# A hybrid decoder trunk on one core: a 25th place for expert weights, a reordered tail, and the third branch's value products a quarter earlier

## The reference

```python
def mixer_block(...):
    xn = rms_norm(x, norm_g)
    proj = xn @ w_in                       # 1024 x (5120 + 8 + 3072)
    y_sb = ...                             # stick-breaking attention, 8 heads x 64
    y_mb = ...                             # block-sparse attention, 8 heads x 64
    y_ml = mlstm_chunkwise(...) * sigmoid(ml_o)   # matrix memory, 4 heads x 128
    y = jnp.einsum("nbsw,nwd->nbsd", branches, w_branch)      # 3 x (512 x 1024)
    merged = jnp.einsum("bsnd,nbsd->bsd", gates, y)
    return x + merged @ w_out

def hier_moe_block(...):
    xn = rms_norm(x, norm_g)
    # softmax over 4 groups takes one; softmax over its 8 experts takes two
    hid = silu(einsum("nd,edf->nef", xn, w1)) * einsum("nd,edf->nef", xn, w3)
    hid = hid * combine                    # 32 experts, inner width 256
    return x + einsum("nef,efd->nd", hid, w2)
```

## Time and profile before

| | us |
|---|---|
| median of 3 executions | 991.89 |
| lowest and highest | 991.26, 992.02 |
| the profiled execution, whole | 992.2 |
| its span in the profile | 990.1 |
| PE busy in the span | 946.0 (96%) |
| PE weight loads | 758.8 (77%) |
| DVE busy | 483.8 (49%) |
| ACT busy | 419.2 (42%) |
| POOL busy | 27.1 (3%) |
| moved by DMA | 293.36 MB |

### The profile page before, as it was taken

One profiled execution on the slowest core, in us unless ns is written; L12 is line 12 of the kernel. 1 busy time (PEld: TensorE's weight loads), 2 busy tenths in 40 slices (PEclk: granted clock), 3 DMA queues, 4 the chain that ended last, 5 costly groups with the idle time before them and its releaser, 6 DMA issues.

```text
span 990.1 us, 19050 instructions
## 1 busy us (share of the span) xinstructions
PE 946.0 (96%) x8004; PEld 758.8 (77%) x8004; DVE 483.8 (49%) x894; ACT 419.2 (42%) x645; POOL 27.1 (3%) x43
## 2 busy tenths in 40 slices
PE   8999999999999999977999999999999999998886
PEld 8898899999876566544698988999998756564544
DVE  7466875477833222222273669655687422232111
ACT  7465654656542221111275565564754421211111
POOL 1011000000000000000100110000000000000000
PEclk9999999999999999989999999999999999999989
DMA  8734545557799999999975264536769999999995
GB/s 288 272 126 170 177 171 170 192 193 298 290 391 402 422 421 420 419 420 421 382 242 198 87 218 157 185 128 213 274 237 365 381 389 421 420 420 420 420 421 212
DMA packets 86310, 293.36 MB, mean 296 GB/s; under 512 B 17040, under 2 KB 17104, under 8 KB 61904
## 3 DMA queue, kind: packets, MB, share of 16 engines
q1 hardware_dynamic: 86224, 292.12, 76.8%
HBM read 291.05 MB, written 1.05 MB: 295 GB/s over the span
## 4 chain that ended last, share of the span: by engine, by line
PE 75%; DMA 14%; DVE 4%; ACT 3%; SPq 1%; issue 1%; ACTq 0%; DVEq 0%
PE ps_a L854 10%; PE ps_a L856 10%; PE ps_a L855 10%; PE ps_b L1186 9%; DMA units_over_xnT<-in_w_dram 6%; PE ps_a L838 5%; PE ps_a L840 5%; PE ps_a L839 5%; PE ps_b L1207 4%; PE ps_b L1134 3%; DMA unit_from_layer_begin<-in_w_dram 3%; DMA weight_ring<-in_w_dram 3%; DMA units_over_splits<-in_w_dram 3%; PE ps_b L1299 2%; PE ps_a L1258 2%; SPq L605 1%
## 5 line engine op out<-in xcount | busy, mean ns | idle before, releaser
L1614 DVE TENSOR_TENSOR w_low<-weight_ring,w_high 128x1024 fp32r<-128x1024 f32 x167 | 201.3, 1230 | 91.9 <-ACT w_high L1330 91.4
L1330 ACT ACTIVATE w_high<-weight_ring 128x1024 fp32r<-128x1024 f32 x166 | 173.6, 1057 | 156.4 <-PE ps_a L856 107.2
L854 PE MATMUL ps_a<-xnT_high,w_high 128*128 128x256 f32 x704 | 200.8, 285 | 0.1
L856 PE MATMUL ps_a<-xnT_high,w_low 128*128 128x256 f32 x704 | 199.0, 283 | 0.0
L855 PE MATMUL ps_a<-xnT_low,w_high 128*128 128x256 f32 x704 | 198.1, 281 | 0.0
L854 PEld LDWEIGHTS ps_a<-xnT_high,w_high 128*128 128x128 f32 x704 | 132.8, 189 | 2.4 <-issue 2.4
L855 PEld LDWEIGHTS ps_a<-xnT_low,w_high 128*128 128x128 f32 x704 | 133.1, 189 | 0.5 <-issue 0.5
L856 PEld LDWEIGHTS ps_a<-xnT_high,w_low 128*128 128x128 f32 x704 | 131.9, 187 | 0.0
L1540 ACT ACTIVATE h<-ps_b 128x256 f32<-128x256 f32 x64 | 24.5, 383 | 142.9 <-PE ps_b L1186 142.9
L1993 DVE TENSOR_TENSOR y_lo<-ps_b,y_hi 128x512 fp32r<-128x512 f32 x30 | 20.8, 692 | 105.8 <-ACT y_hi L1571 105.8
L1299 PEld LDWEIGHTS ps_b<-fold_two_matrices,h 128*128 128x128 f32 x256 | 35.0, 196 | 40.3 <-issue 36.1
(11 more groups left out here) (372 smaller groups left out, 1758.7 us busy)
## 6 DMA issues: line engine op xcount, KB each, us to landing
weight_ring<-in_w_in_dram SPq DMA_DIRECT2D x62, 1024.0 KB, 5.2
units_over_splits<-in_w_dram SPq DMA_DIRECT2D x48, 1024.0 KB, 23.1
units_over_attention<-in_w_dram SPq DMA_DIRECT2D x40, 1024.0 KB, 21.9
weight_ring<-in_w_dram SPq DMA_DIRECT2D x24, 1024.0 KB, 20.8
units_over_xnT<-in_w_dram SPq DMA_DIRECT2D x20, 1024.0 KB, 22.4
units_over_merged<-in_w_dram SPq DMA_DIRECT2D x16, 1024.0 KB, 24.3
weight_ring<-in_w_branch_dram SPq DMA_DIRECT2D x12, 1024.0 KB, 5.4
unit_from_layer_begin<-in_w_dram SPq DMA_DIRECT2D x10, 1024.0 KB, 18.4
```

The costliest lines, as they stand in the source:

```text
L854: mm(dst, wh, xh, start=row == 0 and s % 2 == 0, stop=False, skip_group_check=True)
L856: last = mm(dst, wl, xh, start=False, stop=row == rows - 1, skip_group_check=True)
L1330: A(mix_buf(whi, i), mix_raw(i), ACT.Copy).then_inc(hi_ready, 1)
L1614: v.tensor_tensor(mix_buf(wlo, i), mix_raw(i), mix_buf(whi, i).bitcast(F32), ALU.subtract).then_inc(lo_ready, 1)
```

## The change

The change has six parts.

1. **A 25th place.** `ONCE_UNITS` becomes `(4, 5, 23, 24)`. The new place `unit_over_choice` lies over tiles of the router and over four constants (`tri`, `neg_mask`, `trineg_r`, `negones_r`) and `w_router`, which are moved next to each other for it. It takes the unit with order number 24, a w2 matrix. SP loads it after `unit_over_x`, waiting for the first of the weighted selections (`selw_ready`, DVE line 1919), and before it reads the number of rounds. The loop then has 71 loads.
2. **Constants again.** Since the place overwrites the four constants, POOL builds them again in layer 1 (`constants_again`, eight instructions on tiles of 128x128), and PE and DVE wait for them (`begun` at 11) before they use them.
3. **Moved tiles.** `selectT0` now lies in the place of unit 5 too, so ACT copies it only in the pair p = 1 (`first_selT_out`, waiting until unit 5 is used), and in that pair `outputs(0)` stands before the gathers. The tiles `hid`, `h`, `silu_h1` and `h3_weighted` move elsewhere.
4. **Tail.** `last_y` of the first half comes before the last scatter, and the `idle_work(3)` before that scatter and the `idle_work(2)` before `last_y` are gone (five matmul groups in all).
5. **`ml_out`** moves a quarter earlier, to stand after quarter 1 of branch 1.
6. **Layer 1's first part.** POOL makes `w_low` of the first part in two instructions of half the size, the second of them only after all of the new x is scaled (`xs_ready`), and DVE's wait for it moves one step later.

```diff
-ONCE_UNITS = (4, 5, 23)
+ONCE_UNITS = (4, 5, 23, 24)
+CONSTANTS_AGAIN = 11
...
+    once_choice = Region(nc, one_b.at, whole.at).sb("unit_over_choice", [P, UNIT])
...
-            steps.append(("first_selT", 0))
             selecting.extend((1, piece, 0) for piece in range(3))
+        elif p == 1:
+            steps.append(("first_selT_out", 0))
+            outputs(p - 1)
+            gather()
...
         hidden_T(2 * p + 1)
         if last:
+            steps.append(("last_y", (len(order), 0)))
             steps.append(("scatter", p - 1))
         select_next()
-    steps.extend(("last_y", (len(order), half)) for half in range(2))
+    steps.append(("last_y", (len(order), 1)))
...
                 load_unit(sp, ONCE_UNITS[2])
+                sp.wait_ge(selw_ready, 1)
+                load_unit(sp, ONCE_UNITS[3])
...
+    def constants_again(pool):
+        def below(buf, row, fill):
+            nc.gpsimd.affine_select(out=buf[:, :], in_=buf[:, :], compare_op=ALU.is_ge, fill=fill, base=0,
+                                    pattern=[[row, P]], channel_multiplier=-row).then_inc(begun, 1)
...
-            nc.gpsimd.tensor_tensor(mix_buf(wlo, 0), mix_raw(0), mix_buf(whi, 0).bitcast(F32),
-                                    ALU.subtract).then_inc(lo_ready, 1)
-
-            pool.wait_ge(xs_ready, NT)
+            for k in range(2):
+                if k:
+                    pool.wait_ge(xs_ready, 2 * NT)
+                low = nc.gpsimd.tensor_tensor(mix_buf(wlo, 0)[:, k, :], mix_raw(0)[:, k, :],
+                                              mix_buf(whi, 0)[:, k, :].bitcast(F32), ALU.subtract)
+            low.then_inc(lo_ready, 1)
...
+        if l:
+            pool.wait_ge(lo_ready, 10)
+            constants_again(pool)
...
-        branch(1, [1, 2]); ml_out(); branch(1, [3]); branch(2)
+        branch(1, [1]); ml_out(); branch(1, [2, 3]); branch(2)
...
-                pe.wait_ge(first_taken, 2)
+                pe.wait_ge(first_taken, 1)
...
-                    if p == PAIRS - 2:
-                        idle_work(3, ps_h)
...
                     if half == 0:
-                        idle_work(2, ps_h)
...
-                elif what == "first_selT":
+                elif what == "first_selT_out":
                     act.wait_ge(first_given, 2)
+                    act.wait_ge(unit_used, used[ONCE_UNITS[1]])
...
-        if l:
-            dve.wait_ge(lo_ready, 1)
         for b in range(4):
+            if l and b == 1:
+                dve.wait_ge(lo_ready, 1)
...
+            if l:
+                dve.wait_ge(begun, CONSTANTS_AGAIN)
```

45 lines of the change are left out of this document (30 added, 15 removed).

## The result

The changed kernel took 982.71 us (median of 4 executions, 982.44 to 984.56) beside 991.58 us for the kernel before (4 executions, 989.42 to 992.02): a ratio of 0.9902 with a 95% interval of 0.9882 to 0.9923.

The account below looks back on a forecast made before the run. DMA streams were taken to bound the expert stretches, chained waits between engines the mixers. Gains of 1.6 (ml_out), 2.45 (place), 0.2 (tail) and 0.1 (layer 1's start) sum to 4.35 us: 987.5 us from 991.89, range 985.0 to 990.4.

Parts of the forecast that it names:

- ml_out: Mixer of each layer: moving it a quarter earlier removes PE's wait before branch 2, 0.79 us a layer, 1.6 in all.
- The place: Expert streams: the 25th place fills dips where loads wait on `unit_used`, 2.45 us in all, bounds 0 and 5.0.
- The tail: End of each layer: reordered last steps without idle matmuls gain 0.2 us, all in layer 1, bounds 0 and 0.4.
- Layer 1's start: Start of layer 1: halving POOL's 2.38 us instruction frees DVE's first sum of squares sooner, 0.1 us gained.
- The constants: Layer 1: POOL's eight rebuilding instructions lie beside other work and cost 0, at most 1.5 us.
- the upper bound of that step: Constants in layer 1: one DVE split held up by the whole length of its POOL neighbour, 1.5 us.
- The place gives nothing: Rival, expert streams: dips come from slow transfers, not a missing place, so 990.0 us; chance 0.15.
- The change does not do what it says: Rival, expert loads: the place's wait comes too late and holds back the reloads; result between the first two rivals; no separate chance.
- A whole unit: Rival, expert streams: each stream starts one unit ahead, 5.0 us in place of 2.45, so 985.0 us; chance 0.13.
- The clock: Rival, both tails: PE idling drops the clock, matmuls take twice as long, 10.4 us more, so 997.9 us; chance 0.06.
- whether a stream makes up a dip by itself: Expert streams: a 435 GB/s ceiling could let a 1 us dip vanish, but the windows stayed at 414 to 418.

Follow-up runs that it names:

- One number: Kernel before with region `one` 36992 bytes long instead of 36960, so the two regions behind it start at multiples of 64: 989.02 us, ratio 0.9965.
- the fourth group: Runs on addresses at multiples of 256: changed kernel with old tail 978.65 us, also without the 25th place 980.40, old kernel 985.02; and gather first in changed kernel 982.77.
- The rest alone: Changed kernel with the ml_out move, the 25th place and the new tail all taken back: 981.91 us, ratio 0.9898.

## Why the prediction was wrong

**`ml_out`: right, a little small.** The step said 0.79 us a layer and that a wait of PE's goes. It is 0.93 to 1.08 in the traces of both pairs of kernels that differ in it alone. The step bounded the gain by the wait that the profile names, and two things in PE's row were not as it took them. In the unchanged kernel the last matmul before branch 2 and its first are 1.07 us apart in their starts, in the kernel that moves `ml_out` alone they are 0.44 us apart. A short wait stays (0.2 us; 0.3 in the changed kernel), and 0.63 us go. And there was a second, smaller pause before quarter 2 of branch 1: 0.40 us between the starts (243.16 and 243.56), and 0.12 when `ml_out` stands there. The two give 0.92 of the measured 0.98. By medians the move is worth 1.2 us in the old kernel and 0.5 in the changed one.

**The place: the step failed.** It said that every dip is time in which a load waits for a place, that one more place covers each, and that the early `outputs(0)` works on the same dips and so is not counted again. What happens is the last part turned round: the early outputs shorten the dips (4.7 to 2.7 us over both layers, in means of profiles), and the place on top of them does no more (3.3). With 24 places the changed kernel took 983.46 us, with 25 983.86. The step had the new load "just in front" of the first reload and the queue covering the rest. But the load goes out at 300.95, 5.6 us after `unit_over_x` at 295.34, and that is 0.47 us ahead of the time at which the first reload would have gone without it. It took 6.9 us from issue to landing, with only two units in flight when it was issued (they land at 302.61 and 305.05). So the place puts its 2.5 us of work into the queue when the reload would have come anyway. That an earlier load of the place would fill the first dip is likely by these rows, but no run tried it.

The step also said that every load of the loop now waits for the unit 22 back. By the code that holds for 21 loads: the place takes one unit in a layer, and from unit 46 on a load waits for the unit 21 back, as before. This changes nothing for the dips, which lie early.

**The tail: the mechanism was right, the price was not.** PE idles 1.4 us before `last_y`, the clock holds, and the chain is as long as before within 0.1 us: from `outputs(14)` to layer 1's first projection it is 15.40 us with the new tail and 15.32 with the old one, both from profiled executions of one chip, and in layer 1 to the last copy of the result 10.29 and 10.23. The first copy there ends 0.2 us later and not earlier. So the 0.2 us of gain did not come. Three pairs of medians say 2 to 3 us of loss. In the profiled pairs 0.9 to 1.2 us of it stand in the writes at the end and 0.5 to 1.2 in the stream of layer 1, which no step of the tail touches; the cause of neither is known. The kernel before has the slow writes, too (5.7 and 5.2 us), so of what the change gave nothing was lost there.

**Layer 1's start: as said.** DVE's sum is 0.84 us shorter, but a later sum then waits 0.59 us for ACT, and POOL's second half ends when PE wants it. From `outputs(14)` to the first projection the stretch is 0.1 us shorter in all (15.36 and 15.28 us by the starts of the matmuls).

**The constants: as said.** POOL's eight instructions take 3.3 us, from 510.41 to 513.71, and PE first uses one of them at 549 us. The last one lies beside one of DVE's splits (512.34 to 513.57). The split took its usual 1.23 us, and the POOL instruction 1.31 us; in the profiles where no split runs beside it the same one takes 0.29. So it was POOL that was held up, not DVE as the upper bound of that step feared.

**What was missing: the addresses.** The forecast read the diff's moved tiles as moves without a price, and costed each instruction and each transfer at the duration that it had before. This is the step that failed for most of the gain: a term put at nothing without a reason. Two things changed with the addresses. Both are seen in kernels that differ in nothing else:

1. The mixer's matmuls. Layer 1's stretch from its first ring load behind 490 us to the load of `unit_over_scores` took 242.9 us in the old placement and 241.0 to 241.5 in the four others that were tried in the old kernel. One number (36960 to 36992) gave 3.1 us. That the matmuls themselves follow each other quicker is in the table of the fourth group; why, is open.
2. The stream. A unit that goes to a multiple of 256 takes 2.44 us, to any other of the addresses tried (32, 64, 128, 160 or 192 above a multiple of 256) 2.47 to 2.49. In the changed kernel 9 of 25 places are of the first kind: the mean spacing without the late units fell from 2.485 to 2.464 us, and 0.021 x some 140 units of the two streams = 2.9 us. By medians it is less sure: taking it away again in the changed kernel (`whole.part(32)`) cost 1.0 us, with mixers 0.3 to 0.4 us quicker each.

The Trainium skill ("DMA: Bandwidth & Descriptors", "How a descriptor splits into AXI transactions") says that a transaction has to start at a 256-byte boundary, so that a descriptor which does not start at one gets a first transaction from the boundary below; in its table one of 576 bytes goes from three transactions to four. It speaks of what a transaction reads, and here the side that is written changed. The measured spacings agree in kind: 1.8% more for every start that is not such a multiple, whether 32 or 192 bytes off.

Added up: 3.1 (operands) + 2.9 (places) + 2.0 (`ml_out`, by the traces) + 1.4 to 2 (the dips, by the early outputs) is 9.4 to 10 us, where 8.9 were measured at first and 8.4 and 9.1 on two other chips. The profiled executions, two of the kernel before and three of the changed one, give nearly the same by stages (means):

| stage | us shorter |
|---|---|
| layer 0, start to the load of `unit_over_scores` | 2.2 |
| from there to the landing of its last unit | 2.6 |
| from there to layer 1's first ring load behind 490 us | -0.4 |
| layer 1, from there to the load of `unit_over_scores` | 2.6 |
| from there to the landing of its last unit | 2.6 |
| from there to the end | -0.1 |
| sum, spans of 990.8 and 981.3 us | 9.5 |

The mixers' 4.8 are near 3.1 + 2.0, and the streams' 5.2 are near 2.9 and the dips. The rest alone gave 10.7 us, more than the whole. In its profile the mixers are 1.9 us longer than in the changed kernel, the stretch behind the last landing 1.3 us shorter (the writes) and the streams 1.6 us shorter; the last two are not explained.

**The rivals.** "The place gives nothing" was right about the place, for a reason that was not named (the load comes too late), and wrong about the time. "The change does not do what it says" has a part in it: the reloads do go out later with the place, by 0.87 us. "A whole unit" came nearest in time and is refuted by the kernel without the place; that the time came near it was chance. The clock did not fall. On whether a stream makes up a dip by itself, which the forecast left to the windows: the units behind a dip land 2.48 to 2.49 us apart in the kernel before, as all others, so it did not.

## What to carry to other kernels

A change that moves buffers changes the speed of instructions and transfers that it does not touch: print the old and the new address of every large tile, modulo 512, and the distances between the operands of the same matmuls, and give the difference a term of its own, with a run in which addresses alone change. If a kernel is bound by a stream of transfers, put their targets at multiples of 256 bytes first; here that, with the operands moved along, gave 7.4 us in the old kernel for two lines of padding and one moved tile. And an extra buffer is worth only what its load is earlier by: look at when the load can be issued against when the next load would go out anyway, not at the size of the buffer.

## What was not expected of the hardware

- A transfer of 1 MB in 128 rows of 8 KB into SBUF took 2.44 us at the pace of the stream when each row began at a multiple of 256 bytes, and 2.47 to 2.49 us otherwise; 32 and 128 bytes off are not told apart beyond 0.02 us.
- The same matmuls in the same order ran layer 1's mixer of 243 us 1.4 to 1.9 us quicker when `xnT` and `branchT_parts` lay otherwise to `w_high` and `w_low`. At a distance of 96 above a multiple of 512 both kinds were slow (121.7 and 235.8 ns from start to start); 160 gave the `by_feature` kind 119.6 ns, and 256 gave the `by_token` kind 228.8 ns and left the other at 121.6. Other distances, and the cause, were not tried.
- Beside a DVE split of 1.23 us an instruction of GpSimd took 1.31 us in place of 0.29, and the split was no longer than elsewhere.
- Two tails of equal length up to the last copy differ by 1.2 us in when the last write of the result lands (5.35 and 4.11 us behind its first issue), and one of the four issues takes 1.43 us on SP in place of 0.46.
